# Rows spread over groups of eight, and the last column added by one-hot products instead of scattered: a hybrid encoder layer with 32 experts

## What is computed

```python
p_group = softmax(x @ w_rg + b_rg);  g_w, g_idx = top_k(p_group, 1)
p_exp = softmax(e_logits of that group); e_w, e_idx = top_k(p_exp, 2)
e_w = e_w / sum(e_w);  weights = e_w * g_w
y = sum over the two experts of weight * ((silu(x @ w_gate[e]) * (x @ w_up[e])) @ w_down[e])
out = rmsnorm(h_res + y, final_norm)[16:]
```

## Time and profile before

| | |
|---|---|
| median of 3 runs | 555.13 us (553.97 to 555.59) |
| profiled execution | 552.92 us |
| its span, first to last instruction | 550.8 us |
| PE, DVE, ACT, POOL busy | 483.1, 246.5, 153.0, 40.0 us |
| moved by DMA | 142.69 MB, mean 259 GB/s |
| mean granted TensorE clock | 0.965 of full speed |

### The profile page before, as it was taken

The page is one execution under the profiler, slowest core; times in us unless marked ns, Lnnn a source line. Parts: engine busy times, 40 slices in busy tenths (PEclk is TensorE's granted clock), DMA queues, the critical chain, the costliest instruction groups (busy, mean ns, idle before and its releaser), DMA issues. The chain is left out here.

```text
span 550.8 us, 11000 instructions
## 1 busy us (share of the span) xinstructions
PE 483.1 (88%) x4551; PEld 307.8 (56%) x4551; DVE 246.5 (45%) x608; ACT 153.0 (28%) x377; POOL 40.0 (7%) x47
## 2 busy tenths in 40 slices
PE   3999999999999999999999999999999796657700
PEld 3885478875556655557466565655555454434300
DVE  3206995868236864623574433323232222122237
ACT  5410004766013622422044322222221121011123
POOL 0010000000001000000110011211112011000000
PEclk9999999999999999999999999999999998898965
DMA  7990000000006798007889999999999999999465
GB/s 266 363 353 1 2 0 2 0 1 1 1 2 220 261 422 332 39 39 281 342 277 386 339 417 386 405 414 414 417 414 415 413 412 417 410 417 411 196 260 213
DMA packets 38754, 142.69 MB, mean 259 GB/s; under 512 B 5170, under 2 KB 12584, under 8 KB 30384
## 3 DMA queue, kind: packets, MB, share of 16 engines
q1 hardware_dynamic: 31824, 127.89, 59.0%
q0 software_dynamic: 5760, 11.55, 6.0%
q10 hardware_dynamic: 1120, 2.54, 1.2%
HBM read 135.83 MB, written 15.20 MB: 274 GB/s over the span
## 5 line engine op out<-in xcount | busy, mean ns | idle before, releaser
L1457 PE MATMUL bank<-area_w,area_m 128*128 128x512 f32 x128 | 58.5, 609 | 0.4 <-issue 0.4
L1569 PE MATMUL bank<-area_g,area_m 128*64 128x256 f32 x352 | 42.7, 385 | 3.9 <-DMA area_g<-in_w_exp_up 3.9
L764 DVE SCALAR_TENSOR_TENSOR area_m<-area_g,cols,area_m 128x512 f32<-128x512 f32 x60 | 39.8, 743 | 0.0
L1457 PEld LDWEIGHTS bank<-area_w,area_m 128*128 128x128 f32 x128 | 24.1, 195 | 27.5 <-issue 27.5
L1569 PE MATMUL bank<-area_w,area_m 128*64 128x256 f32 x256 | 30.8, 383 | 7.6 <-DMA area_w<-in_w_exp_up 7.3
L1288 PE MATMUL bank<-area_h,area_w 128*128 128x264 f32 x160 | 35.9, 386 | 0.0
L1569 PEld LDWEIGHTS bank<-area_g,area_m 128*64 128x64 f32 x352 | 23.9, 136 | 19.4 <-issue 8.0
L1783 DVE COPY cst<-bank 128x128 f32<-128x128 f32 (+1 forms) x39 | 10.2, 260 | 54.8 <-PE bank L1586 29.8
L1288 PEld LDWEIGHTS bank<-area_h,area_w 128*128 128x128 f32 x160 | 30.4, 190 | 5.6 <-issue 0.5
L1322 PE MATMUL bank<-area_h,area_w 128*128 128x512 f32 x64 | 30.8, 612 | 0.0
L1569 PEld LDWEIGHTS bank<-area_w,area_m 128*64 128x64 f32 x256 | 18.2, 137 | 18.3 <-issue 11.0
(11 more groups left out here) (357 smaller groups left out, 769.3 us busy)
## 6 DMA issues: line engine op xcount, KB each, us to landing
area_w<-in_w_exp_gate SPq DMA_DIRECT2D x14, 1024.0 KB
area_w<-in_w_exp_up SPq DMA_DIRECT2D x14, 1024.0 KB
area_g<-in_w_exp_gate SPq DMA_DIRECT2D x14, 1024.0 KB, 16.4
area_g<-in_w_exp_up SPq DMA_DIRECT2D x14, 1024.0 KB, 23.7
area_g<-in_w_exp_down SPq DMA_DIRECT2D x14, 1024.0 KB, 22.7
area_w<-in_w_exp_down SPq DMA_DIRECT2D x14, 1024.0 KB, 22.4
area_w<-in_w_in SPq DMA_DIRECT2D x7, 1024.0 KB, 12.6
area_w<-in_w_out SPq DMA_DIRECT2D x2, 2048.0 KB, 12.5
```

The source lines that it names most:

```text
L764: ins = V.scalar_tensor_tensor(out=mixT[:, i, :], in0=src, scalar=w, in1=mixT[:, i, :], op0=ALU.mult, op1=ALU.add)
L1457: ins = T.matmul(bank[7][:, :], mixT[:, k, j * P:(j + 1) * P], w_out_sb[:, n, k, :], start=(k == 0), stop=(k == KT - 1))
L1569: ins = T.matmul(out_b[h * BC:(h + 1) * BC, 0:2 * P], x[:, k, :], w_gate_up[slot][:, :, k, h * P:(h + 1) * P], start=(k == 0), stop=(k == ...
```

## The change

1. **Rows of a block.** A token of rank k in a block of n rows sits in row 8 (k mod n/8) + k div n/8: neighbours in rank are eight rows apart. This holds for early blocks, for the picked column and, by arithmetic on the word in `places`, for all others (of 32, 64 or 128 rows).
2. **Last column.** Column 16 is no longer scattered. From the one-hot rows of that column, weighted, VectorE builds four 128x128 matrices (`last_rows`, during blocks 20 to 23), TensorE turns them (after block 24), and after block 41 eight products of them with the column's results give each token's share in eight PSUM banks. The weights are split: `w_rest` for what is read back, `w_last` for the last column, `w_spare` for the loop.
3. **Read back.** `rows_back` is issued by SyncE alone, both results of a tile after one another, once columns 0 to 15 have landed. VectorE makes the sums of all four tiles, then adds the eight banks, then norms all four tiles.
4. **Fill.** As rows of `expert_out` may now be read that nobody wrote, SyncE first writes 4 MB of finite numbers (weights of slot 2) over it, after slot 2 has landed, before the scatter of column 0.
5. **Last two blocks.** For blocks 40 and 41, TensorE does turn and down product of the block before first, then all of gate and up. ScalarE alone takes out the last block's results.
6. **Final gain.** Its load on GpSimd's queue goes behind the scatter of column 9, since the one-hot rows live in its place until then.
7. Eight semaphores are merged in pairs, and the loop for tokens without a row gets its own read back and sums.

The core of the diff:

```diff
+LAST = len(PLAN) - 1
+MIX_AT = 20
+GAIN_AFTER = min(i for i, n in enumerate(END_OF) if n >= MIX_AT + NT)
...
+            sp.wait_ge(d_gu[2], 32)
+            for k in range(2):
+                sp.dma_start(expert_out[k * SEQ:(k + 1) * SEQ, :].rearrange("(p j) d -> p (j d)", p=P),
+                             slot_of[2][:, PIECE:3 * PIECE]).then_inc(d_fill, 16)
...
+            def spread(at_iota, n):
+                return cst[:, at_iota:at_iota + n].rearrange("p (r e) -> p e r", r=8).unsqueeze(1)
...
+                mark(V.tensor_scalar(by_four, word, 2, 127, ALU.logical_shift_right, ALU.bitwise_and))
+                mark(V.tensor_scalar(more_by, word, 10, 3, ALU.logical_shift_right, ALU.bitwise_and))
...
+                mark(V.tensor_tensor(eighth, by_four, more_by, ALU.logical_shift_right))
+                mark(V.tensor_scalar(rows_less, cq, 32.0, -1.0, ALU.mult, ALU.add))
...
-                mark(V.scalar_tensor_tensor(out=row_f, in0=rq, scalar=32.0, in1=rk, op0=ALU.mult, op1=ALU.add))
+                mark(V.tensor_tensor(rows_less, rows_less, eighth, ALU.mult))
+                step(V.scalar_tensor_tensor(out=row_f, in0=rk, scalar=8.0, in1=rows_less, op0=ALU.mult, op1=ALU.subtract))
+                mark(V.scalar_tensor_tensor(out=row_f, in0=rq, scalar=32.0, in1=row_f, op0=ALU.mult, op1=ALU.add))
...
+                mark(V.tensor_tensor(w_spare, w12, in_spare, ALU.mult))
+                step(V.tensor_tensor(w_last, w12, in_last, ALU.mult))
+                step(V.tensor_tensor(w_rest, w12, w_last, ALU.subtract))
+                step(V.tensor_tensor(w_rest, w_rest, w_spare, ALU.subtract))
+
+            def last_rows(j):
+                step(V.tensor_scalar(mix[:, j, :], slot_is[:, 0, j, :], w_last[:, 0, j:j + 1], None, ALU.mult))
+                V.scalar_tensor_tensor(out=mix[:, j, :], in0=slot_is[:, 1, j, :], scalar=w_last[:, 1, j:j + 1], in1=mix[:, j, :],
+                                       op0=ALU.mult, op1=ALU.add).then_inc(mix_made, 1)
...
         def sent_in_all(u):
-            return 16 * len(range(u, len(PLAN), 2))
+            return 16 * len(range(u, LAST, 2))
...
+            for u in range(2):
+                sp.wait_ge(d_sc[u], sent_in_all(u))
+            rows_back(sp)
...
+                for j in range(NT):
+                    for n in range(2):
+                        T.matmul(bank[MIX_BANK[j][n]][:, :], mix_flat[0:LAST_ROWS, j * P:(j + 1) * P],
+                                 yb[LAST % 2][0:LAST_ROWS, n * 512:(n + 1) * 512], start=True, stop=True).then_inc(mixed, 1)
...
+            for b_ in (NB - 2, NB - 1):
+                act_turn(b_ - 1)
+                out_of(b_ - 1)
+                gate_up_first(b_)
+                gate_up_second(b_)
             act_turn(NB - 1)
             out_of(NB - 1)
+            last_rows()
```

176 lines of the change are left out of this document (112 added, 64 removed).

## The result

| | before | after |
|---|---|---|
| median, first comparison | 555.36 us (4 runs) | 564.75 us (4 runs) |
| ratio, 95% interval | | 1.0143 (1.0093 to 1.0193) |
| median, second comparison | 556.37 us (17 runs) | 563.92 us (6 runs) |
| ratio, 95% interval | | 1.0122 (1.0070 to 1.0174) |
| profiled execution, its span | 552.92, 550.8 | 565.13, 563.3 |

The kernel is slower by 7.6 to 9.4 us by the medians; the intervals of the ratios allow 4 to 11 us. The prediction said slower (74%) and 559.6, with 554.0 to 562.5 as its range: the sign was right, the size too small, the time outside the range.

The account below looks back on a forecast made before the run. The weight stream was taken as the bound, its end set by the busiest DMA engine. First pair -1.0 (spread +3.8 and gain +0.5 included) and sums +5.5 gave +4.5: 555.13 to 559.6 us, range 554.0 to 562.5.

Parts of the forecast that it names:

- What bounds the kernel: Weight stream at its end: the busiest DMA engine, some 8 us behind the mean, sets what PE waits for.
- The spread, +3.8: Rows of blocks: 209 instead of 185 rows on the busiest DMA engine, 0.159 us each, end the stream 3.8 us later.
- Final gain, +0.5: Its load moves into the full stream: 1.3 us late, 0.8 won back at the start, net +0.5 us.
- Fill 0: Writing 4 MB over expert_out, 10.2 us of stream, costs nothing, hidden in the DMA hole between 216 and 249.
- index arithmetic and one-hot products 0: Extra VectorE operations in places and blocks 20 to 23 cost 0 while loads stay backlogged, otherwise 2 to 4 us.
- The mixing products: Eight PE products after the last block: 0.609 us each, twice that at half clock, ending by 537 with 5 us spare.
- Last two blocks 0: Reordered PE work in blocks 40 and 41 costs 0; column 15's scatter leaves some 4 us sooner, near 514.
- Read back and first pair: Tail: the first pair takes 2.5 us behind the residual rows, landing at 531.4 against 532.37, a gain of 1.0 us.
- Sums, +5.5: VectorE's tail: sums, eight new PSUM additions and norms take 21.4 us instead of 15.9, so +5.5 us.
- rival 3: Slower gathers and a late scatter of column 15 lengthen the tail: +7 to +8, 563 us; chance 6%.
- Rival 1: Engines take rows in eights, so the spread evens them out and the stream ends near 516: 547.7 us; chance 14%.
- rival 2: The spread moves nothing because rows without a token take no place: +0.7, 555.8 us; chance 10%.

Follow-up runs that it names:

- fours: The changed kernel with its rows spread over groups of four instead of eight: 548.86 us, 552.09 us when run again (0.9896 and 0.9898 of before).
- groups of two: The changed kernel with its rows spread over groups of two instead of eight: 550.14 us, 0.9874 of before.
- experiment 4: The changed kernel with a wait bounding the lead of SyncE's loads to two experts: 566.77 us; the same wait with groups of four rows: 551.45 us.
- (3): The changed kernel with late rows of odd columns moved by four within their group of eight: 549.33 us, 0.9903 of before.
- (2, 5): Changed kernel with groups of sixteen rows: 564.41 us, of 32: 563.74 us, of two: 550.14 us; kernel before with groups of four alone: 550.15 us.
- after in rank order: The changed kernel with a token's rank as its row again, all else kept: 558.27 us, 1.0034 of before.

## Why the prediction was right and wrong

**What bounds the kernel: right.** The stream, and in it the busiest DMA engine. The share of 0.57 and 0.40 at the end, the landing 28.1 us after issue, and the gain of 13.2 us by fours bear it out. One part was wrong: 4 us by which the mean engine was less far ahead than counted I put down to light engines running dry. The count was too long: the runs fit rows that count from about 350, where the stream is full for good, and not from 305 (groups of two, and 52 rows or 8.2 us for the 8.5 measured).

**The spread, +3.8: the term that was mis-sized; it measured +6.7** (in the kernel before +7.5). The count itself was right in the difference (24 rows by the one, 25 by the other count, 4.0 us). The step that failed is the price of a row on the busiest engine, 0.159 us with the stream at 413 GB/s throughout. The rate of the full stream falls when rows pile up on half of the engines and the others are light: 4.7 us of full work lost from 400 to 505, and the landing 2.7 us behind what the count gives. The run with alternating columns, which has neither, shows that it is the sum over the stream that does it. I had looked for light engines that run dry and called that harmless. That they catch up with SyncE's issue is an inference, and why about half of the lost rate reaches the busiest engine stays open: the distance between engines is not it (experiment 4), nor is the unevenness of single transfers (3), nor which engines are heavy (2, 5).

**Final gain, +0.5: 1.2 to 1.6**, measured with groups of four. It costs its full weight; nothing came back at 304. That and some 0.4 not accounted for make L of after in rank order 1.7 longer than before.

**Fill 0, index arithmetic and one-hot products 0: right for the fill**, by 10.2 us written twice for at most 0.8. The arithmetic shows nowhere: from the first weight load to the index lists it is 106.7 us in before (190.85 to 297.51), in before with groups of eight (191.21 to 297.94) and in after (194.78 to 301.45). The one-hot products were not run alone. The mixing products were put at 0.61 each, twice that at half clock, to end by 537; they took 10.17 us for the eight, from 535.65 to 545.8 (the clock was 0.50 from 535 to 540), 6 us behind the first sum and still ahead of the additions at 550.2.

**Last two blocks 0: not shown alone in this kernel.** The scatter did not leave near 514 and land near 520: it was issued at 521.3 (3.9 of that by chance), and the read back at 529.7. What covers it (to 528.9 in the prediction) is the late landing itself. Where the landing is early, the order is worth about 3 us.

**Read back and first pair: right.** 2.7 us behind the landing (2.5 predicted), so no overlap beyond that.

**Sums, +5.5: +4.5, and +0.8 behind them.** 8 additions took 4.87 and not 5.5, the norms 5.0 and not 5.3. All norms at the end leave the output later: 3.3 us from VectorE's end instead of 2.5; with all sums on PE, where the norms stand between the additions, it is 2.5 again (543.96 to 546.5). Together 5.3.

**Sum.** Predicted +4.5; L is 4.2 more (2.9 from the spread, the rest from the gain and what stays unaccounted for), the tail 0.1 less: +8.5 by S. Forecast and rival 3 had the sign; rival 3's price (+7 to +8) was near, its mechanism (column 15's scatter too late) not the cause. Rival 1 (eights to an engine) and rival 2 (the spread moves nothing) are refuted by the runs with groups of four and of eight alone.

**What was asked of the profile of after:** landing 30 us or more after issue (28.1: no); a share of 0.25 to 0.3 at the end (0.40 from 525 to 530 with part of column 15's scatter in it, 0.26 from 529 to 530: yes, for the last us); first pair near 531 (539.6, of it 3.9 chance); 8 additions between sums and norms, and VectorE without a gap (yes).

## What to carry to other kernels

Count the rows of indirect transfers by DMA engine over the whole full stream, not per transfer: here neighbours in rank belong four rows apart (126 rows on the busiest engine and 549 us, against 209 and 564 with eight), and even an uneven spread costs nothing if it alternates. Before a step is hidden behind a late landing, ask what it is worth once the landing is early: the reordered last blocks, put at nothing here, were worth about 3 us once the stream was even. And measure stage against stage from a mark behind the part that varies by chance: medians told 7.6 or 9.4 us; two marks in the trace told 8.5, and the second profile of after repeated it within 0.1.

## What was not expected of the hardware

- Rate and share part: 1.00 and 390 GB/s from 455 to 505 in after, 1.02 and 414 before. A share near 1 does not show that the engines deliver.
- Bounding the lead of SyncE's loads to two experts is free on an even stream (416 GB/s, L 222.6); on an uneven one 9.2 us of full work are lost from 400 to 505 where 4.7 were without it, and the landing is 1.9 later.
- A 128x512 product costs PE two matmuls of 0.43 us (13.90 us for 32) where I had taken the mean of one row, 0.61, for a whole product.
- The granted clock from 180 to 200 was 1.00 in twelve profiles and 0.74 to 0.84 in eight, in a part of the program where all do the same work; the place of all that follows varied by up to 8 us.
